# Issuing the stores of the turned outputs from ScalarE's queue instead of SyncE's, in a retention and HGRN2 layer on one core

## The reference

```python
proj = h @ w_in
rq, rk, rv, rg, hq, hf_f, hf_b, hi, hg = jnp.split(proj, N_IN_PARTS, axis=-1)
...
o_r = merge(rms_norm(o_rf + _flip(o_rb))) * jax.nn.silu(rg)
...
o_h = merge(rms_norm(o_hf + _flip(o_hb), hg_norm_w)) * jax.nn.silu(hg)
out = jnp.concatenate([o_r, o_h], axis=-1).astype(x.dtype) @ w_out
x = x + (gate[:, None, :] * out).astype(x.dtype)
```

## Time and profile before

| | |
|---|---|
| median of 3 runs | 1410.25 us (1410.1 to 1410.5) |
| the profiled execution | 1410.22 us |
| its span, first to last instruction | 1408.2 us |
| PE busy | 1391.7 us, 99% |
| DVE busy | 992.9 us, 71% |
| ACT busy | 487.0 us, 35% |
| POOL busy | 373.2 us, 27% |
| transfers | 204.00 MB, mean 145 GB/s |

### The profile page before, as it was taken

The page is one execution under the profiler, slowest core; times in us unless marked ns, Lnnn a source line. Parts: engine busy times, 40 slices in busy tenths (PEclk is TensorE's granted clock), DMA queues, the critical chain, the costliest instruction groups (busy, mean ns, idle before and its releaser), DMA issues.

```text
span 1408.2 us, 24739 instructions
## 1 busy us (share of the span) xinstructions
PE 1391.7 (99%) x10106; PEld 1172.4 (83%) x10106; DVE 992.9 (71%) x1314; ACT 487.0 (35%) x866; POOL 373.2 (27%) x292
## 2 busy tenths in 40 slices
PE   7999999999999999999999999999999999999997
PEld 5788898889888988898889888988898888888886
DVE  5555676667689888878888888876676668632345
ACT  4323243334333333342334233333333344221234
POOL 0000115311532153215321532153215216201220
PEclk9999999999999999999999999999999999999999
DMA  9994242324343534353435443433333347183235
GB/s 389 417 419 160 81 124 75 99 57 139 93 157 82 171 99 163 80 161 109 154 83 157 128 145 97 134 98 90 85 103 92 90 136 276 47 302 100 91 105 209
DMA packets 168438, 204.00 MB, mean 145 GB/s; under 512 B 110080, under 2 KB 118544, under 8 KB 163472
## 3 DMA queue, kind: packets, MB, share of 16 engines
q1 hardware_dynamic: 168304, 202.50, 44.7%
q10 hardware_dynamic: 32, 0.02, 0.0%
HBM read 178.08 MB, written 20.20 MB: 141 GB/s over the span
## 4 chain that ended last, share of the span: by engine, by line
PE 95%; DMA 3%; DVE 1%; SPq 0%; issue 0%; ACT 0%; DVEq 0%; ACTq 0%
PE ps L2086 10%; PE ps L2087 10%; PE ps L2088 10%; PE ps L1910 9%; PE ps L1911 8%; PE ps L1912 8%; PE ps L1886 8%; PE ps L2268 5%; PE ps L2270 5%; PE ps L2269 5%; DMA area<-in_w_mod 3%; PE ps L2103 2%; PE ps L1917 2%; PE ps L1918 2%; PE ps L1919 2%; PE ps L1876 2%
## 5 line engine op out<-in xcount | busy, mean ns | idle before, releaser
L1172 DVE TENSOR_TENSOR w_lo<-area,w_hi 128x1024 fp32r<-128x1024 f32 x143 | 188.0, 1315 | 212.9 <-ACT w_hi L697 212.9
L697 ACT ACTIVATE w_hi<-area 128x1024 fp32r<-128x1024 f32 x143 | 151.5, 1059 | 492.6 <-PE ps L2088 263.2
L2086 PE MATMUL ps<-w_hi,hT_hi 128*128 128x512 f32 x640 | 251.4, 393 | 0.0
L2088 PE MATMUL ps<-w_hi,hT_lo 128*128 128x512 f32 x640 | 249.2, 389 | 0.0
L2087 PE MATMUL ps<-w_lo,hT_hi 128*128 128x512 f32 x640 | 249.2, 389 | 0.0
L1910 PE MATMUL ps<-hT_hi,w_hi 128*128 128x512 f32 x512 | 205.1, 401 | 0.0
L1912 PE MATMUL ps<-hT_hi,w_lo 128*128 128x512 f32 x512 | 199.7, 390 | 0.0
L1911 PE MATMUL ps<-hT_lo,w_hi 128*128 128x512 f32 x512 | 199.7, 390 | 0.0
L2088 PEld LDWEIGHTS ps<-w_hi,hT_lo 128*128 128x128 f32 x640 | 120.1, 188 | 25.4
L2086 PEld LDWEIGHTS ps<-w_hi,hT_hi 128*128 128x128 f32 x640 | 120.2, 188 | 24.6
L2087 PEld LDWEIGHTS ps<-w_lo,hT_hi 128*128 128x128 f32 x640 | 120.2, 188 | 24.1
(11 more groups left out here) (286 smaller groups left out, 2443.4 us busy)
## 6 DMA issues: line engine op xcount, KB each, us to landing
area<-in_w_in SPq DMA_DIRECT2D x144, 512.0 KB, 4.2
area<-in_w_mod SPq DMA_DIRECT2D x26, 1024.0 KB, 12.4
area<-in_w_out SPq DMA_DIRECT2D x38, 512.0 KB, 3.8
gate_raw<-in_w_gate SPq DMA_DIRECT2D x32, 512.0 KB, 3.7
gate_raw<-in_w_mod SPq DMA_DIRECT2D x6, 1024.0 KB, 12.1
o_hi_scratch<-area SPq DMA_DIRECT2D x56, 80.0 KB, 2.4
o_lo_scratch<-area SPq DMA_DIRECT2D x56, 80.0 KB, 2.4
hT_hi<-o_hi_scratch SPq DMA_DIRECT2D x14, 320.0 KB, 6.9
```

Of the source, the lines that this page charges most:

```text
L697: act.activation(split_weights(h, n)[0], raw[:, n % 3, :], ACT.Copy).then_inc(wt_hi.sem, 1)
L1172: v.tensor_tensor(lo, raw[:, n % 3, :], hi.bitcast(F32), ALU.subtract).then_inc(wt_lo.sem, 1)
L2086: mm(out, hT_hi[:, k, tile_cols(t)], w_hi[:, n % 2, w], start=k == 0, stop=False)
L2088: i = mm(out, hT_lo[:, k, tile_cols(t)], w_hi[:, n % 2, w], start=False, stop=k == KT - 1)
```

## The change

`store_turned` moves from SP's program to ScalarE's with nothing altered but the issuing engine. The retention group, which SP issued in slot 8, is issued by ScalarE in slot 7, behind the split of chunk 8; the HGRN2 group, which SP issued in slot 17, is issued by ScalarE in slot 16, behind L885. The waits for `o_split` move with them.

```diff
@@ SP @@
-            def store_turned(row, stored):
-
-                for dram, buf in ((o_hi_dram, o_two), (o_lo_dram, o_one)):
-                    out = dram[bass.ds(row, 1)].rearrange("h (c i) (t q j) -> q i (h t) c j", c=QUARTERS, q=QUARTERS, j=QUAD)
-                    for q in range(QUARTERS):
-                        sp.dma_start(out[q], buf[q * QUAD:(q + 1) * QUAD, :].rearrange("p (t c j) -> p t c j", c=QUARTERS, j=QUAD)
-                                     ).then_inc(stored.sem, 16)
-
...
                 if n == 8 and prev is not None:
-                    sp.wait_ge(o_split.sem, o_split.at(prev, 1))
-                    store_turned(prev, r_stored)
                     store_states(prev, n_hg_f, n_hg_b, hst, h_state, h_state_stored)
...
-                if n == 17 and prev is not None:
-                    sp.wait_ge(o_split.sem, o_split.at(prev))
-                    store_turned(prev + HEADS, h_stored)
@@ ScalarE @@
+            def store_turned(row, stored):
+
+                for dram, buf in ((o_hi_dram, o_two), (o_lo_dram, o_one)):
+                    out = dram[bass.ds(row, 1)].rearrange("h (c i) (t q j) -> q i (h t) c j", c=QUARTERS, q=QUARTERS, j=QUAD)
+                    for q in range(QUARTERS):
+                        act.dma_start(out[q], buf[q * QUAD:(q + 1) * QUAD, :].rearrange("p (t c j) -> p t c j", c=QUARTERS, j=QUAD)
+                                     ).then_inc(stored.sem, 16)
+
...
+                    if n == 7:
+                        act.wait_ge(o_split.sem, o_split.at(prev, 1))
+                        store_turned(prev, r_stored)
...
                     scan_factors(h)
+                    if prev is not None:
+                        act.wait_ge(o_split.sem, o_split.at(prev))
+                        store_turned(prev + HEADS, h_stored)
```

## The result

The changed kernel takes 1414.35 us, the median of ten runs (1411.8 to 1414.79), against 1410.22 us (ten runs, 1410.02 to 1410.5) for the kernel before: a ratio of 1.0026, 95% interval 1.0018 to 1.0035, 4.1 us slower. The forecast, 1410.2 with a range up to 1412.7 and "the same" as the likeliest case, did not hold. The profiled execution took 1414.38 us with a span of 1412.5, 4.3 more than before's 1408.2, at a mean granted clock of 0.996 where before had 0.998.

A forecast was written before the change was run, and what follows sets the result against it. PE, busy 1391.7 of 1408.2 us and waiting for neither queue, was taken as the bound. SP's relief and ScalarE's added issues each counted 0, so 1410.22 + 0 = 1410.2 us, range 1409.5 to 1412.7.

The forecast's parts named there:

- PE waited for neither queue: Kernel before: PE busy 1391.7 of 1408.2 us, without a gap where nearly all moved stores lie.
- ScalarE's queue would issue the group ahead of its activations: Slot 16: the group can be issued beside the activations, from about 1.2 us before L885 starts.
- SP's price for the transfer: Each moved issue costs 0.68 us on ScalarE as on SP: 5.5 us a group, 6.2 in heads 3 to 6.
- the cost of 0 in slot 7 and at the ends of heads 1 to 6: Both moved groups there end in time or within the room ahead of PE, costing 0 us.
- 0.65 us of room in the last head: Last head, ahead of PE's L2268: L1299's 0.51 us idle for PE plus 0.14 after its end.
- the next split released by PE in all heads: Sign of being right, behind slot 16: PE releases each next split, 5.3 us after L885's start.
- the last head has 1.0 + 0.65 us in hand: Last head's slot-16 group: 5.5 us ends 1.0 before PE's release; with 0.65 of room, a 1.3 us long issue fits.
- Other parts: Store landings, later waits and SP's earlier reads of stored rows in the last head; no time was added for them.
- upper price, 9.2 us a group: Either slot: 0.99 us an issue on ScalarE, 7.9 a group, 9.2 with a long issue; used for the range.
- C: Rival: the two queues hold each other's issues up, 2.6 us in slot 7, 0.7 in slot 16; 1410.2 or 1411; chance 0.1.
- A: Rival, head ends: ScalarE issues only after its activations, at 0.9 us an issue, delaying the next split; 1419.6 us; chance 0.12.
- B: Rival: earlier loads free PE; 1409.9 us, or 1400 if the gaps ahead of L2103 hung on transfers; chance 0.03.

The follow-up runs named there:

- kernel 1: The change, with the last head's slot-16 group of eight stores issued by SP again: 1409.63 us, ratio 1.0000.
- kernel 4: kernel 1, with the slot-16 groups of heads 1 to 6 issued twice, the second time into scratch that nothing reads: 1438.97 us, ratio 1.0205.
- kernel 3: The change, with SP's reads of rows 4 to 6 and what follows held until the last slot-16 stores have landed: 1409.79 us, ratio 1.0002.
- kernel 5: The kernel before, with only the last head's slot-16 group on ScalarE and an SP wait holding its reads to their old time: 1420.42 us, ratio 1.0073.
- kernel 7: The change, with the last head's four slot-16 stores of o_lo back on SP, ahead of its reads: 1410.40 us, ratio 1.0006.

## Why the prediction was wrong

**Right:** that PE waited for neither queue; that ScalarE's queue would issue the group ahead of its activations; SP's price for the transfer (0.60 to 0.67 us on ScalarE, so 5.5 us a group in a quiet stretch); the cost of 0 in slot 7 and at the ends of heads 1 to 6, which kernel 1 confirms; and 0.65 us of room in the last head, which fits to 0.04 us.

**Right in the sum, wrong in the step:** "the next split released by PE in all heads". In heads 3 to 6 the groups take 6.6 to 7.5 us instead of 6.2, with one or two long issues of 1.0 to 1.8 us each instead of none, and the split follows the group. The room took it. Which way gives first there was misjudged too: kernel 4 shows the first token values, which the prediction didn't price. Why these ordinary long issues occur stays open; they stood in nearly the same places in kernels 1, 3 and 4.

**The step that failed** is in the last head: "the last head has 1.0 + 0.65 us in hand, which a long issue (1.3) fits". The group was priced at 5.5 us plus one long issue and measured 9.9. The reason was in view, under "Other parts": "in the last head SP's reads of stored rows (L589) get earlier". I costed that at nothing, asking only whether the data would be there, and not what the transfers would run into. They are 4.6 MB, and the store issues they met are now ahead of PE's critical split. The earlier trace rows gave an upper end for a long issue, 1.97 us, but from a kernel in which the same queue kept the stores ahead of the reads, so it was no bound for this one. The prediction's upper price, 9.2 us a group, lies near 9.9, but it stood for issues that are dear on ScalarE everywhere, and these take 0.61 to 0.67 us at the median; by it the last head would lose 2.7 - 0.65 = 2.05 us.

**The missing term** is the clock: +1.6 us behind a wait of 2.7. The upper end of the range knew waits of PE, and none of what they can cost afterwards.

**The rivals.** C named a mutual hold-up of the queues and looked for it at the generator, at one of SP's issues each, and counted it as no change; it acts through the transfer engines instead, and where they are full it costs 4.4 us a group, not 0.7. A's first condition (issues only behind the activations) is false in every head. Its second, 0.9 us or more an issue, is met by the mean of a group in heads 4 to 6 (7.3 to 7.5 us for eight, by the long issues in them) and in the last head (9.9 / 8 = 1.24), and not by the ordinary issue. B was rightly small: the gaps ahead of L2103 did not move (9.9 us in 28, as before). Two sums of the prediction are slightly off, and nothing hangs on them: at slot 7's upper price the split would be 2.4 us late (662.92 + 9.2 - 669.72), not 2.5, and A at 0.68 leaves out the four middle heads, 0.4 us.

The Trainium skill (DMA: Bandwidth & Descriptors, Issuing engines are not separate DMA queues) says that transfers started by several engines run on the same 16 transfer engines and interleave, and that spreading them saves only the issuing time, usually small relative to the transfer. The trace agrees on the first half, q1 and q10 sharing the full engines above. On the second it differs for these stores: in kernel 3 one issue takes 0.67 of the 2.4 us until its store has landed, and eight in a row 5.6 us, and it is the issuing time that came to stand in PE's way.

## What to carry to other kernels

Moving issues to another queue takes away an order that the one queue gave for nothing: look at what stood behind them and now starts early, and whether its traffic meets the moved issues at their new place. Price an issue of many small pieces by the load of the transfer engines at that moment. On a computing engine such a group holds the next activation in the program, so place it where neither the load nor a late split matters, or hold the bulk reads until the stores have landed. When PE has no gap, 2.7 us of delay can cost more than 2.7 us: allow for products at half the clock behind the wait, which came behind most waits of 2.5 us or more here, and not behind all.

## What was unexpected of the hardware

The issue of one and the same store, 80 KB in pieces of 128 bytes, took 0.67 us at the median with its own queue alone on the transfer engines (kernel 3), up to 2.4 us with them full (the change) and 1.9 to 4.1 us beside SP's reads (kernels 5 and 7, the later issues of their groups), while SP's own issues of 320 KB reads stayed at 0.4 to 1.1 us in the same time. And a wait of PE has a second price that doesn't follow from its length: at the end of the last head the twelve following products lost nothing behind 0.9 us, 1.6 us behind 2.7, and 2.5 us behind 4.5 and behind 8.4; at the seams of kernel 4 the clock fell to half behind a wait of 2.5 us and stayed at 2.4 GHz behind one of 2.6.
